# The filler matmuls between the stages of a block stack: left out of the norms

## The chip, the cores and the metric

One Trainium2 chip, of which the kernel uses one core. The metric is the device time of the whole program in microseconds. Before the change it is 2915.89 us, the median of three runs (2914.72 to 2917.57).

## The reference

512 tokens of width 1024 in float32 go through two layers of a first block and one layer of a second. Each layer is a feed-forward network, a token mix, and another feed-forward network, every one of them added to the running `x` after a norm:

```
h = modulate(rms_norm(x, g), shift, scale)
x = x + 0.5 * gate * (silu(h @ w_g) * (h @ w_u)) @ w_out        # feed-forward, inner width 2816
x = x + gate * token_mix(h)                                     # projections, spatial gating, sparse attention
```

with `rms_norm(x, g) = x * rsqrt(mean(x*x) + 1e-6) * g`. The second block has the same frame with a recurrent unit and two attentions in its mix, and no modulation. A final norm of the first block stands between the two. A norm needs all of `x`: no product of a stage can start before the norm ahead of it has given its first tile.

## The kernel before, in words

`x` lies transposed in SBUF, as 8 tiles of 128 features by 512 tokens. Every float32 product is done as three float32r matmuls (`pe_3`, lines 318 to 320): the high part of the weights times the high part of the data, high times low, low times high. Weights stream in as units, ScalarE makes their high part (line 290) and VectorE or GpSimd their low part (lines 283, 259). All engines run programs written out in order by hand and meet at counting semaphores; there is no scheduler.

The class `Norm` is one norm between two stages; this document calls the place of one a seam. Its order on TensorE is `pe_sum`, then `pe_spread`:

- The squares of `x` are made on ScalarE (line 389) and seven of eight tiles are added up on VectorE (line 398) while the stage before is still multiplying. `pe_sum` sums over the features with four one-column products of the accumulated tile (line 407) and, once the last tile of squares is there, four more (line 414). They are plain float32, and the trace shows each as two matmuls. Then `keep_warm` issues `warm[1]` matmuls of a constant 128x128 tile with 512 columns (line 313).
- VectorE and ScalarE turn the 512 sums into reciprocal roots (lines 424, 429, 436, and 569 to 576).
- `pe_spread` waits for them, spreads each over the 128 partitions with four products against the identity (line 442), and `keep_warm` issues `warm[2]` more.
- VectorE multiplies `x` by that (line 454), ScalarE makes the high part `hH` of each tile (line 487) and VectorE the low part `hL` (line 461, or 464 without a shift). TensorE starts the stage's products on tile 0 as soon as its `hL` is there, and takes one more tile at a time after that.

The products of `keep_warm` write PSUM bank 2, which nobody reads before the stage overwrites it; nothing waits for them.

The norms are numbered 0 to 9. Norm 0 (`warm=(26, 0, 16)`), the norm of the memory (6), the bridge between the blocks (7) and norm 8 (each `warm=(0, 0, 0)`) name their counts; at 7 and 8 products of a side stage stand where the filler would be. Norms 1, 2, 3, 4, 5 and 9 take the default `warm=(0, 4, 4)`. Their sums start at 397.2, 631.0, 998.9, 1366.9, 1601.3 and 2542.0 us of the profiled execution; they are called seams A to F here. A and D lead into the mix, C and the others into feed-forward networks (B, E, F in front of the second one of a layer, where VectorE also does the two halves of a low part, line 274, between its steps of the norm). `pe_woven`, the first group of products of the program, has its own filler matmuls (line 668).

Of the kernel before, what the change touches and what calls it, by code (L numbers as in the profile page):

```python
# [25 lines left out]
T = 512  # L26
# [332 lines left out]
class Norm:  # L359
# [4 lines left out]
    ADDS = 6  # L364
    SQUARES = KD + 1

    def __init__(self, n, q, a, y0=None, seam=None, tokens=T, src=None, warm=(0, 4, 4), warm_bank=2, banks=(6, 5, 7)):
        self.seam = seam
        self.warm, self.warm_bank, self.banks = warm, warm_bank, banks
        self.n, self.q, self.a, self.y0, self.tokens, self.src = n, q, a, y0, tokens, src or (lambda m, d: m.x[:, d])  # L370
# [2200 lines left out]
```

## Time and profile before

| | |
|---|---|
| median of 3 runs | 2915.89 us (2914.72 to 2917.57) |
| profiled execution, its own time | 2915.27 us |
| its span, first to last instruction | 2913.2 us |
| TensorE busy | 2875.0 us, 99% |
| VectorE, ScalarE, GpSimd busy | 53%, 29%, 8% |
| mean granted TensorE clock | 0.994 |

"PE" is TensorE, "PEld" its weight loads, "DVE" VectorE, "ACT" ScalarE. The granted clock is a share of 2.4 GHz: 1.00 is that, 0.50 is 1.2 GHz. The matmuls are pipelined, so a busy time holds the tail of each: what a matmul costs in a row of them is the distance from its start to the next one's start. In a row "[1.55 <-DVE m_hL L461]" says that the engine was idle for 1.55 us before it and what ended that.

### The profile page before, as it was taken

The numbers are of one execution on the slowest core, as the hardware profiler recorded it, in microseconds if no ns is written. First come the engines' busy times: TensorE is split into PE (matmuls) and PEld (weight loads), VectorE is DVE, ScalarE is ACT, GpSimd is POOL, SyncE is SP. The second block draws the span as 40 slices with busy tenths as digits, with TensorE's granted clock in tenths as the row PEclk, the third lists the DMA queues.
The fourth block names the chain that finished last, engine by engine and source line by source line (L and its number), as shares of the span: only waits on it lengthen the run. The fifth ranks groups of instructions, "written<-read, shape, count | busy, mean of one in ns | idle before, by whom it ended". The sixth has DMA issues, their size and how long they took to land.

```text
span 2913.2 us, 35989 instructions
## 1 busy us (share of the span) xinstructions
PE 2875.0 (99%) x13895; PEld 2372.3 (81%) x13895; DVE 1550.6 (53%) x2217; ACT 855.6 (29%) x998; POOL 237.4 (8%) x107
## 2 busy tenths in 40 slices
PE   8999999999999999999999999999999999999999
PEld 6888887878888888887887788888888878788887
DVE  7654658766533465365686662364423456643232
ACT  4222233442212322123334321243212344432121
POOL 0000005410000000000451000000000014100000
PEclk9999999999999999999999999999999999999999
DMA  6544522125523255353321462222322321123222
GB/s 264 197 159 157 196 98 94 51 88 181 194 72 112 78 186 202 113 183 120 112 69 59 162 220 95 104 105 80 117 82 89 115 89 44 62 99 128 72 96 77
DMA packets 63756, 351.23 MB, mean 121 GB/s; under 512 B 7842, under 2 KB 10274, under 8 KB 36260
## 3 DMA queue, kind: packets, MB, share of 16 engines
q1 hardware_dynamic: 62564, 347.90, 33.5%
q10 hardware_dynamic: 1088, 1.97, 0.4%
q8 instruction: 62, 1.02, 0.1%
q14 instruction: 42, 0.34, 0.0%
HBM read 345.78 MB, written 2.10 MB: 119 GB/s over the span
## 4 chain that ended last, share of the span: by engine, by line
PE 89%; DVE 6%; DVEq 2%; issue 1%; DMA 1%; ACT 1%; SPq 0%; ACTq 0%
PE bank L318 28%; PE bank L320 28%; PE bank L319 28%; DVE m_m L1522 2%; DVEq L1521 1%; PE bank L1128 1%; PE bank L326 1%; PE bank L1105 1%; PE bank L1114 0%; PE bank L442 0%; DVE m_masks L1532 0%; DVE m_masks L1530 0%; DVE m_masks L1524 0%; DVE m_masks L1537 0%; DVE m_mod_big L2105 0%
## 5 line engine op out<-in xcount | busy, mean ns | idle before, releaser
L318 PE MATMUL bank<-m_hH,m_wH 128*128 128x512 f32 x2464 | 967.0, 392 | 13.6 <-DVE m_hL L461 6.4
L320 PE MATMUL bank<-m_hH,m_wL 128*128 128x512 f32 x2464 | 960.5, 390 | 0.0
L319 PE MATMUL bank<-m_hL,m_wH 128*128 128x512 f32 x2464 | 960.2, 390 | 0.0
L283 DVE TENSOR_TENSOR m_wL<-m_wraw,m_wH 128x2048 fp32r<-128x2048 f32 (+3 forms) x185 | 459.9, 2486 | 583.6 <-ACT m_wH L290 583.0
L290 ACT ACTIVATE m_wH<-m_wraw 128x2048 fp32r<-128x2048 f32 (+3 forms) x236 | 459.7, 1948 | 897.4 <-PE bank L320 896.4
L318 PEld LDWEIGHTS bank<-m_hH,m_wH 128*128 128x128 f32 x2464 | 463.4, 188 | 114.5 <-issue 20.3
L320 PEld LDWEIGHTS bank<-m_hH,m_wL 128*128 128x128 f32 x2464 | 463.3, 188 | 97.3
L319 PEld LDWEIGHTS bank<-m_hL,m_wH 128*128 128x128 f32 x2464 | 463.7, 188 | 94.4 <-issue 0.2
L318 PE MATMUL bank<-m_guH,m_wH 128*128 128x512 f32 x1248 | 491.7, 394 | 3.6 <-DVE m_x L1197 2.8
L320 PE MATMUL bank<-m_guH,m_wL 128*128 128x512 f32 x1248 | 485.9, 389 | 0.0
L319 PE MATMUL bank<-m_guL,m_wH 128*128 128x512 f32 x1248 | 485.9, 389 | 0.0
L318 PEld LDWEIGHTS bank<-m_guH,m_wH 128*128 128x128 f32 x1248 | 234.1, 188 | 61.5 <-issue 9.8
L320 PEld LDWEIGHTS bank<-m_guH,m_wL 128*128 128x128 f32 x1248 | 234.2, 188 | 49.1
L319 PEld LDWEIGHTS bank<-m_guL,m_wH 128*128 128x128 f32 x1248 | 234.3, 188 | 46.6
L713 ACT ACTIVATE m_sg<-bank 128x512 f32<-128x512 f32 x132 | 78.7, 599 | 442.0 <-PE bank L320 441.7
L1047 DVE CUSTOM_DVE_ANT_0 m_mod_w<-m_mod_w,m_c 128x1024 f32<-128x1024 f32 x144 | 171.1, 1223 | 25.6 <-DMA m_mod_w<-in_ada_w 11.8
L759 DVE TENSOR_TENSOR m_gut<-m_sg,bank 128x512 f32<-128x512 f32 x132 | 90.8, 688 | 155.4 <-PE bank L320 151.8
L993 DVE SCALAR_TENSOR_TENSOR m_x<-bank,m_gate,m_x 128x512 f32<-128x512 f32 (+1 forms) x68 | 48.3, 717 | 184.4 <-PE bank L320 183.6
L259 POOL TENSOR_TENSOR m_wL<-m_wraw,m_wH 128x1024 fp32r<-128x1024 f32 (+1 forms) x30 | 85.7, 2858 | 234.6 <-ACT m_wH L290 234.6
L763 DVE TENSOR_TENSOR m_guL<-m_gut,m_guH 128x512 f32 (+1 forms) x132 | 91.4, 693 | 16.7 <-issue 0.8
L993 DVE SCALAR_TENSOR_TENSOR m_x<-bank,m_x 128x512 f32<-128x512 f32 (+1 forms) x42 | 27.8, 665 | 133.4 <-PE bank L320 133.1
L2222 POOL MEMSET m_other<- 128x1024 f32 x2 | 1.9, 955 | 1172.9 <-DVE m_wL L283 1172.9
(280 smaller groups left out, 2115.0 us busy)
## 6 DMA issues: line engine op xcount, KB each, us to landing
m_wraw<-in_ffn_in SPq DMA_DIRECT2D x132, 1024.0 KB, 4.8
m_mod_w<-in_ada_w SPq DMA_DIRECT2D x144, 512.0 KB, 4.5
m_wraw<-in_ffn_out_a SPq DMA_DIRECT2D x24, 1536.0 KB, 8.3
m_wraw<-in_ffn_out_b SPq DMA_DIRECT2D x24, 1280.0 KB, 6.1
m_wraw<-in_mix SPq DMA_DIRECT2D x30, 1024.0 KB, 4.8
m_wraw<-in_mix SPq DMA_DIRECT2D x26, 512.0 KB, 3.5
m_mod_big<-in_ada_w SPq DMA_DIRECT2D x16, 512.0 KB, 12.2
m_x<-in_x SPq DMA_DIRECT2D x2, 1024.0 KB, 6.3
```

Of the source, the lines that this page charges most:

```text
L259: nc.gpsimd.tensor_tensor(m.wL[:, j, 0:size], m.wraw[:, j, 0:size], f(m.wH[:, j, 0:size]), ALU.subtract)\
L283: nc.vector.tensor_tensor(m.wL[:, j, 0:size], m.wraw[:, j, 0:size], f(m.wH[:, j, 0:size]), ALU.subtract).then_inc(s.low, 1)
L290: nc.scalar.activation(m.wH[:, j, 0:size], m.wraw[:, j, 0:size], ACT.Copy).then_inc(s.high, 1)
L318: nc.tensor.matmul(out, a[0], b[0], start=first, stop=False)
L319: nc.tensor.matmul(out, a[0], b[1], start=False, stop=False)
L320: return nc.tensor.matmul(out, a[1], b[0], start=False, stop=last)
L713: nc.scalar.activation(m.sg[:, j], m.bank[j][:], ACT.Silu).then_inc(s.silu, 1)
L759: nc.vector.tensor_tensor(m.gut[:, j], m.sg[:, j], m.bank[2 + j][:], ALU.mult).then_inc(s.ufree, 1)
L763: nc.vector.tensor_tensor(m.guL[:, tile + j], m.gut[:, j], f(m.guH[:, tile + j]), ALU.subtract).then_inc(s.gu, 1)
L993: nc.vector.scalar_tensor_tensor(out=m.x[:, d, at], in0=m.bank[4 + d % 4][:, at], scalar=gate(d), in1=m.x[:, d, at], op0=ALU.mult, op1=ALU ...
L1047: return nc.vector.tensor_tensor_reduce(out=w, in0=w, in1=m.c[:], scale=1.0, scalar=0.0, op0=ALU.mult, op1=ALU.add, accum_out=m.red[:, k:k ...
L1522: nc.vector.max(m.m8[:], score[i])
```

## The change

The default of `warm` becomes `(0, 0, 0)`. At the six seams A to F no matmuls of `keep_warm` are issued any more, neither behind the sums nor behind the spreading. Nothing else changes: no wait, no buffer, no other count.

```diff
@@ -364,7 +364,7 @@ class Norm
-    def __init__(self, n, q, a, y0=None, seam=None, tokens=T, src=None, warm=(0, 4, 4), warm_bank=2, banks=(6, 5, 7)):
+    def __init__(self, n, q, a, y0=None, seam=None, tokens=T, src=None, warm=(0, 0, 0), warm_bank=2, banks=(6, 5, 7)):
```

## Rows read from the trace of the kernel before

**Rows 1.** The page: busy time, share and instructions; the chain that ended last.

```profile
PE 2875.0 (99%) x13895; PEld 2372.3 (81%) x13895; DVE 1550.6 (53%) x2217; ACT 855.6 (29%) x998; POOL 237.4 (8%) x107
PE 89%; DVE 6%; DVEq 2%; issue 1%; DMA 1%; ACT 1%; SPq 0%; ACTq 0%
```

**Rows 2.** Line 313 alone, first of six seams: start:end, length, PE, PEld busy (count).

```profile
397.22:404.33 7.11, 2.35 (x8) 1.36 (x8) 1.00 0.00 0
...
```

**Rows 3.** Timeline of TensorE at seam A: start, length, instructions, [idle before].

```profile
397.22 0.95 PE L407 MATMUL bank<-m_ones,m_acc 128*128 128x1 f32 x8
398.40 1.05 PE L414 MATMUL bank<-m_ones,m_sq 128*128 128x1 f32 x8 [0.24 <-ACT m_sq L389]
399.32 1.18 PE L313 MATMUL bank<-m_warm 128*128 128x512 f32 x4
400.69 1.16 PE L442 MATMUL bank<-m_cst,m_nr 128*128 128x128 f32 x8 [0.20 <-DVE m_nr L576]
401.61 1.17 PE L313 MATMUL bank<-m_warm 128*128 128x512 f32 x4
404.33 0.47 PE L318 MATMUL bank<-m_hH,m_wH 128*128 128x512 f32 x1 [1.55 <-DVE m_hL L461]
```

**Rows 4.** Timeline of VectorE at seam A.

```profile
400.48 0.17 DVE L576 SCALAR_TENSOR_TENSOR m_nr<-m_nv,m_nt 128x4 f32<-128x4 f32 x1
...
```

**Rows 5.** Seams A to F, first sum to first product: length, busy by engine, granted clock.

```profile
397.22:404.33 7.11, 5.12 (x34) 4.03 (x32) 4.18 (x12) 3.35 (x6) 0.00 (x0) 1.00 0.00 0
631.02:639.65 8.63, 6.47 (x33) 5.04 (x32) 6.61 (x15) 4.20 (x6) 0.00 (x0) 0.80 0.27 84
998.92:1006.94 8.02, 6.63 (x34) 5.32 (x32) 4.17 (x12) 4.20 (x6) 0.00 (x0) 0.79 0.36 131
1366.92:1374.54 7.62, 6.41 (x33) 4.91 (x32) 4.17 (x12) 3.34 (x6) 0.00 (x0) 0.78 0.00 1
1601.30:1609.05 7.75, 5.12 (x33) 4.02 (x32) 6.61 (x15) 4.19 (x6) 0.00 (x0) 1.00 0.18 48
2542.00:2550.18 8.18, 6.45 (x34) 5.22 (x32) 6.26 (x14) 4.13 (x6) 0.00 (x0) 0.79 0.25 88
```

**Rows 6.** The stretches at half clock, same columns (PE busy first).

```profile
15.79:22.61 6.82, 5.92 (x18) 5.05 (x19) 6.41 (x13) 2.27 (x5) 0.00 (x0) 0.50 1.03 420
29.44:36.26 6.82, 5.86 (x14) 4.63 (x15) 6.72 (x9) 1.11 (x2) 0.00 (x0) 0.50 1.03 406
633.60:637.01 3.41, 3.03 (x12) 2.23 (x11) 2.31 (x7) 2.00 (x2) 0.00 (x0) 0.50 0.00 0
1002.24:1005.65 3.41, 3.26 (x12) 2.87 (x12) 1.24 (x3) 1.52 (x2) 0.00 (x0) 0.50 0.36 145
1370.88:1374.29 3.41, 2.89 (x11) 1.98 (x9) 2.05 (x3) 1.38 (x2) 0.00 (x0) 0.50 0.01 2
2446.08:2449.49 3.41, 3.41 (x11) 2.61 (x10) 3.26 (x5) 0.28 (x1) 1.39 (x1) 0.50 0.00 0
2545.07:2548.48 3.41, 2.96 (x12) 2.60 (x12) 2.23 (x6) 1.62 (x1) 0.00 (x0) 0.50 0.15 26
```

**Rows 7.** Timeline of TensorE at seam C.

```profile
1002.39 2.08 PE L442 MATMUL bank<-m_cst,m_nr 128*128 128x128 f32 x8 [0.20 <-DVE m_nr L576]
1004.12 1.87 PE L313 MATMUL bank<-m_warm 128*128 128x512 f32 x4
1006.94 0.47 PE L318 MATMUL bank<-m_hH,m_wH 128*128 128x512 f32 x1 [0.95 <-DVE m_hL L461]
```

**Rows 8.** Timeline of TensorE inside the mix of the second block.

```profile
2445.00 0.66 PE L1646 MATMUL bank<-m_cst,m_other 128*128 128x128 f32 x4 [2.19 <-ACT m_other L1605]
...
2446.70 0.63 PE L319 MATMUL bank<-m_hL,m_wH 128*128 128x512 f32 x1
2447.13 0.63 PE L320 MATMUL bank<-m_hH,m_wL 128*128 128x512 f32 x1
```

**Rows 9.** TensorE's waits: who waited for whom, total us, times, longest.

```profile
PE bank L318 <- DVE m_hL L461: 6.4, 5, 1.5
```

## The prediction

> **What bounds the kernel now.** I read the page first: TensorE is busy 99% of the span, and 89% of the chain that ended last is its products [rows 1]. Whatever delays the first product of a stage, or makes products slower, therefore goes into the time nearly one to one; the rest of the chain is a search on VectorE that starts only when TensorE's first products after a norm are done. Then I took the seams. At seam A [rows 3] the stage's last product gives way to the sums at 397.22 and the next stage's first product starts at 404.33. The seam is a chain over three engines: sums until 399.45, VectorE's last reciprocal root from 400.48 to 400.65 [rows 4], spreading from 400.69, then a tile of `x` through VectorE, ScalarE and VectorE until its low part `hL` is there. The filler matmuls lie in the two holes of this chain. Third, the granted clock of the six seams [rows 5] and the stretches in which it was 0.50, 1.2 in place of 2.4 GHz [rows 6]: with the filler in place the clock already falls at B, C, D and F, and stays up at A and E.
>
> **What goes, and what it frees.** Eight matmuls a seam [rows 2] (the other five seams have eight each too), 48 in all. Counted by their work this would be up to 48 x 1.18 / 4 = 14 us [rows 3]. None of it is on the path. At A the first four end (399.32 + 1.18 = 400.50) 0.19 us before the spreading, which waits for VectorE; the second four end at 402.78, 1.55 us before the first product, which waits for `hL` [rows 3]. At C, where the second four run at half clock, they end at 1005.99 and the first product still waits 0.95 us for `hL` [rows 7]. They are issued behind the sums and the spreading, so they delay neither signal. The direct gain is 0; from the other side it can hardly be more than the 0.2 us of idle before the spreading, whose weight load may have been held up a little, 6 x 0.2 = 1.2 us at most. SP, GpSimd, every wait and every buffer are untouched.
>
> **What late products cost now.** The clock fell 2.58, 3.32, 3.96 and 3.07 us after the first sum of B, C, D and F (633.60 - 631.02 and so on, rows 5 and 6), mean 3.23. That is about when the spreading starts, and it pays: 2.08 us at C against 1.16 at A [rows 3, 7]. So the first product comes later: C 8.02 against A 7.11, B 8.63 against E 7.75 (both with VectorE's extra work), D 7.62 against A 7.11 [rows 5]. A fall costs 0.91, 0.88, 0.51. At all four the clock was back at full before the first product or within its time: the half stretches lasted 3.41 us, and TensorE worked 2.89 to 3.26 us of each, a good part of it filler (at C from 1004.12 on, rows 7).
>
> **What they cost afterwards.** Without the filler TensorE does only sums and spreading between 397.2 and 404.3: from 399.45 to 400.69 it is idle (1.24 us), and from 401.85 to 404.33 (2.48 us). An idle time of 2.19 us was enough for a fall within the mix (2445.00 in [rows 8], the stretch from 2446.08 in [rows 6]), and B, C, D and F fell even with the filler. I take it that the clock falls at all six.
>
> (a) Late spreading at A and E, which are spared now: 2 x 0.9 = 1.8 us. At B, C, D and F this is paid already.
>
> (b) Products at half clock. A product there costs 0.43 us from start to start (2446.70 to 2447.13, rows 8) and half of that at twice the clock (the page's 2875 us over 13,895 matmuls gives 0.21, rows 1), so half of the time spent so is lost. How long does it last? Where TensorE had paused for about one us in the half stretch, it lasted 6.82 us (5.92 and 5.86 busy, the two early rows of rows 6). In the seams afterwards TensorE will have the spreading, 2.05 us, then 2.75 us of idle, so less work than in any stretch of rows 6. Lower end: 3.41 us as now, the clock is back before the first product and (b) is 0. Next: 6.82 us, so until 3.23 + 6.82 = 10.05 us after the first sum; the first product is at 8.1 (mean of B, C, D, F), 1.95 us run at half clock, 0.97 us lost. Upper end: one 3.41 us more, since even in 6.82 us there are only 2.05 + 1.95 = 4.0 us of work, less than the 5.9 of the two early ones: until 13.5, 5.4 us at half clock, 2.7 lost. I take the middle of the last two, 1.85 us, because the pause lies differently to the stretch from seam to seam. Six seams: 11.1 us. No slack takes the loss: TensorE waited for a tile's `hL` five times at the five seams A to E, the first tile's each time (6.4 us in all), and never for a later one [rows 9]; at full clock it is the later of the two already, and at half clock the more so.
>
> Sum: 1.8 + 11.1 = 12.9 us on the profiled execution's own 2915.27 (span 2913.2 and 2.1 around it) = 2928.2; that execution lies 0.6 us under the median of the runs, so **2928.8 us**.
>
> The Trainium skill bears on this (TensorE: Matmul & The Clock Gate, "Why this matters for your kernels"): it advises against idle gaps above some 3 us between bursts of matmuls, and by that rule gaps of 1.2 and 2.5 us would be harmless. That speaks against my sum. The trace does not agree: the gap of 2.19 us was followed by a fall [rows 8]. What is worked out from rows for this case is the third rival below.
>
> **Rivals.** *One stretch only.* The clock falls everywhere but is back after 3.41 us: only (a), 2917.7. For it: every half stretch after the first 40 us was so long [rows 6]. Against it: TensorE worked 2.89 us or more in each, and here it would be the 2.05 us of spreading.
>
> *Always the long one.* 6 x 2.7 + 1.8 = 18.0, so 2933.9; for it that the two early long stretches had more work than these will have.
>
> *The gaps are harmless, the other side.* If falls hang on something else than on the filler's work (on long idle times, say, or a matter of chance), they come no more often than now: 2915.9; and if the plain gaps of a seam never drop the clock, the late starts of B, C, D and F vanish, 0.9 x 3 + 0.5 = 3.2 us, which gives 2912.7. It decides from the point where a seam keeps granted clock 1.00 with the two gaps of 1.2 and 2.5 us. For it: A kept it, with gaps of 0.20 and 1.55 us. Against it: C fell with gaps of 0.20 and 0.95 us [rows 3, 7].
>
> **Chances.** A measurement of this kernel tells 0.2% (5.8 us) from no change. Forecast, 2922 to 2932: 0.62. Always long, to 2936: 0.18. One stretch only, 2917.7, within 0.2%: 0.09. Harmless, 0.11, nearly all of it within 0.2% too, 0.02 faster by more. So slower 0.80, same 0.18, faster 0.02. The range is 2918 to 2935: the lower end is the first rival, the upper the second with a fall that comes a little earlier.
>
> **What the changed profile would show.** Line 313 with 63 matmuls for 111; rows of seam A with 0.50 in the clock and the spreading at 2.1 us; the gap before the first product some 2.5 us or more; then products 0.43 us apart for 2 to 5 us at each seam, and the mean granted clock at about 0.988 for 0.994 (six stretches of 7 to 10 us for four of 3.4). VectorE's first `hL` comes 0.9 us later at A and E and not at C. I am wrong if the half stretches still last 3.4 us, or if the clock stays at 1.00 at A and E; and wrong in another way if the time is there but lies outside the 15 us behind the seams.

## The result

The changed kernel takes 2926.96 us, the median of six runs (2925.55 to 2930.3), against 2916.56 us for the kernel before in six (2914.51 to 2917.57): 10.4 us more by the medians. The ratio on record, 1.0038 with a 95% interval of 1.0027 to 1.0050, is not the ratio of these two medians (that is 1.0036); here and below the interval belongs to the ratio. The forecast was 2928.8 us (+12.9) and slower. Run once more beside another kernel, it took 2926.21 us against 2917.24, ratio 1.0036, interval 1.0022 to 1.0049.

The profiled execution took 2926.91 us, its span is 2924.9 us, 11.7 us more than before, and the mean granted clock is 0.989 for 0.994. The head of the page and line 313 alone:

```profile
span 2924.9 us, 35893 instructions
PE 2869.3 (98%) x13847; PEld 2368.7 (81%) x13847; DVE 1550.3 (53%) x2217; ACT 855.1 (29%) x998; POOL 237.4 (8%) x107
L313 PE MATMUL bank<-m_warm x63: 387/393/792, 3.3 to 53.2; 128*128 128x512 f32 x63
```

TensorE does 48 matmuls less, all others do the same work, and the program is longer. Seam A in the timeline of TensorE, to be held against [rows 3]:

```profile
397.67 0.95 PE L407 MATMUL bank<-m_ones,m_acc 128*128 128x1 f32 x8
398.86 1.05 PE L414 MATMUL bank<-m_ones,m_sq 128*128 128x1 f32 x8 [0.24 <-ACT m_sq L389]
401.15 1.16 PE L442 MATMUL bank<-m_cst,m_nr 128*128 128x128 f32 x8 [1.24 <-DVE m_nr L576]
404.78 0.77 PE L318 MATMUL bank<-m_hH,m_wH 128*128 128x512 f32 x1 [2.47 <-DVE m_hL L461]
405.34 0.63 PE L319 MATMUL bank<-m_hL,m_wH 128*128 128x512 f32 x1
```

The spreading comes 3.48 us after the first sum and the first product 7.11, both as before; only the idle times have grown, from 0.20 to 1.24 and from 1.55 to 2.47 us (the tail of a filler matmul used to count as busy). What is new is the length of the first product, 0.77 us for 0.47: it runs at half clock. Below, a fall is a change of the granted clock from 1.00 to 0.50, and a half stretch is the time that it then stays at 0.50. The six seams from the first sum to the first product, as in [rows 5]:

```profile
397.67:404.77 7.10, 3.16 (x25) 2.82 (x24) 4.16 (x12) 3.34 (x6) 0.00 (x0) 0.87 0.00 0
633.79:642.07 8.28, 3.68 (x26) 3.24 (x24) 6.61 (x15) 4.19 (x6) 0.00 (x0) 0.78 0.23 70
1002.71:1010.01 7.30, 3.35 (x25) 2.91 (x24) 4.17 (x12) 4.20 (x6) 0.00 (x0) 0.80 0.43 144
1371.17:1378.29 7.12, 3.16 (x26) 2.82 (x24) 4.17 (x12) 3.34 (x6) 0.00 (x0) 0.82 0.00 1
1606.92:1615.49 8.57, 3.97 (x26) 3.54 (x24) 6.61 (x15) 4.19 (x6) 0.00 (x0) 0.75 0.25 84
2552.50:2560.26 7.76, 3.66 (x26) 3.22 (x24) 6.26 (x14) 4.13 (x6) 0.00 (x0) 0.77 0.23 72
```

Their half stretches, as in [rows 6]:

```profile
402.86:409.69 6.83, 4.91 (x12) 3.88 (x13) 6.70 (x11) 3.95 (x6) 0.00 (x0) 0.50 0.00 0
638.39:645.20 6.81, 4.34 (x15) 3.39 (x14) 6.04 (x10) 3.35 (x5) 0.00 (x0) 0.50 0.73 269
1007.03:1013.84 6.81, 4.33 (x12) 3.29 (x12) 6.14 (x10) 3.63 (x6) 0.00 (x0) 0.50 0.04 14
1375.67:1382.48 6.81, 4.34 (x12) 3.35 (x11) 6.50 (x10) 3.55 (x5) 0.00 (x0) 0.50 0.00 1
1611.18:1621.42 10.24, 7.77 (x22) 6.24 (x23) 9.17 (x14) 5.23 (x8) 0.00 (x0) 0.50 0.55 207
2556.68:2563.48 6.80, 4.39 (x14) 3.44 (x14) 6.05 (x10) 3.48 (x6) 0.00 (x0) 0.50 0.43 154
```

All six seams fall, and each stretch is 6.8 or 10.2 us long where it was 3.4; it reaches 3.1 to 5.9 us into the products. Their price can be read off directly. These rows run from the first product of a seam to the start of the 48th (the columns count line 318 alone, one in three of the 48), of the kernel before for seams A and E:

```profile
404.33:415.10 10.77, 6.30 (x16) 2.97 (x16) 1.00 0.01 2
1609.05:1619.83 10.78, 6.32 (x16) 2.97 (x16) 1.00 0.39 163
```

and of the changed kernel for all six:

```profile
404.77:417.86 13.09, 7.32 (x16) 3.55 (x16) 0.81 0.17 56
642.07:654.32 12.25, 7.07 (x16) 3.35 (x16) 0.87 0.34 130
1010.01:1022.56 12.55, 7.08 (x16) 3.50 (x16) 0.85 0.07 12
1378.29:1391.01 12.72, 7.20 (x16) 3.50 (x16) 0.84 0.14 44
1615.49:1629.05 13.56, 7.57 (x16) 3.64 (x16) 0.78 0.36 134
2560.26:2572.57 12.31, 7.10 (x16) 3.36 (x17) 0.87 0.15 52
```

Before, the six such stretches take 64.6 us together (10.73 to 10.78 each), afterwards 76.5: 11.9 us lost in products. The seams ahead of them take 47.3 us before [rows 5] and 46.1 now: 1.2 us won back. Together +10.7 of the span's +11.7 us. The rest lies elsewhere and partly cancels: ahead of seam A the program is 0.45 us longer, between the products of C and the sums of D 0.6 us shorter, and between the products of E and the sums of F 1.3 us longer. In that last part, inside the mix of the second block, which the change does not touch, a half stretch that was 3.41 us long before (from 2388.05 on) is 6.83 us long now (from 2396.24 on), and the one from 2446.08 on in [rows 6] is gone.

### The profile page after: what moved, and what is told of

The parts are those of the page before. It is cut to its first block, busy times and chain, and to the rows that moved or that the text cites. A ratio compares the mean times of both kernels' runs of the same rounds, so it can differ in the third digit from the quotient of the medians.

```text
span 2924.9 us, 35893 instructions
## 1 busy us (share of the span) xinstructions
PE 2869.3 (98%) x13847; PEld 2368.7 (81%) x13847; DVE 1550.3 (53%) x2217; ACT 855.1 (29%) x998; POOL 237.4 (8%) x107
## 4 chain that ended last, share of the span: by engine, by line
PE 89%; DVE 7%; DVEq 2%; issue 1%; ACT 1%; DMA 0%; SPq 0%; ACTq 0%
PE bank L318 29%; PE bank L319 28%; PE bank L320 28%; DVE m_m L1522 2%; DVEq L1521 1%; PE bank L1128 1%; PE bank L326 1%; PE bank L1105 1%; DVE m_mod_big L2105 1%; PE bank L1114 0%; DVE m_masks L1532 0%; DVE m_masks L1530 0%; DVE m_masks L1524 0%; PE bank L442 0%; DVE m_masks L1537 0%
```

## The experiments

Each is timed against the kernel before on the same chip; the second column of the table is the difference of the two medians in us, the third the ratio with its 95% interval, most of them some 2.6 us (0.09%) to either side. The last column comes from one profile each: the six seams and the 48 products behind each, together, less the same in the profile of the kernel before (47.3 + 64.6 = 111.9 us). It leaves out what changes elsewhere in the program.

| kernel | us | ratio | at the seams, us |
|---|---|---|---|
| changed kernel again | +9.0 | 1.0036 (1.0022 to 1.0049) | +11.5 |
| e1: filler behind the sums only | +7.4 | 1.0025 (1.0016 to 1.0035) | +10.7 |
| e2: filler behind the spreading only | +1.3 | 1.0005 (0.9996 to 1.0014) | +6.3 |
| e3: both holes filled, 5 and 10 | -0.4 | 0.9999 (0.9990 to 1.0008) | +0.4 |
| e4: eight thin filler matmuls | +10.0 | 1.0043 (1.0030 to 1.0057) | +12.3 |
| e5: left out at seam A alone | +0.5 | 0.9999 (0.9990 to 1.0008) | +1.9 |
| e6: 1 inside the sums, 5 and 6 | -4.3 | 0.9982 (0.9973 to 0.9991) | -3.2 |
| e7: 3 inside the sums, 5 and 6 | -3.7 | 0.9988 (0.9979 to 0.9997) | -2.2 |
| e8: 0 and 8 | +1.9 | 1.0010 (1.0001 to 1.0020) | +2.6 |
| e9: 1 inside the sums, 4 and 4 | -3.9 | 0.9988 (0.9979 to 0.9997) | -2.7 |

**Do the matmuls count, or their work?** (e4)

```diff
     for _ in range(n):
-        nc.tensor.matmul(m.bank[bank][:], m.warm[:], m.warm[:].unsqueeze(1).to_broadcast([P, TT, P]), start=True, stop=True)
+        if n == 4:
+            nc.tensor.matmul(m.bank[bank][:, 0:16], m.warm[:], m.warm[:, 0:16], start=True, stop=True)
+        else:
+            nc.tensor.matmul(m.bank[bank][:], m.warm[:], m.warm[:].unsqueeze(1).to_broadcast([P, TT, P]), start=True, stop=True)
```

> The eight filler matmuls of each of the six seams are issued, but with 16 columns in place of 512. Theory (their work counts, not that they are issued): as the changed kernel, +8 to +13 us, half stretches of 6.8 us or more at all six seams. Rival (any stream of instructions on TensorE's queue keeps it ready): as the kernel before, within 2 us.

+10.0 us: as if they were not there, though all 48 and their weight loads are issued. The rival that any stream on the queue will do has fallen. All six seams have half stretches of 6.83 or 10.24 us in its profile; those of A and B:

```profile
400.48:410.72 10.24, 8.42 (x26) 7.10 (x27) 8.01 (x12) 4.40 (x7) 0.00 (x0) 0.50 0.00 0
639.41:646.24 6.83, 5.01 (x17) 4.08 (x16) 6.49 (x11) 3.62 (x6) 0.00 (x0) 0.50 0.80 302
```

**Which of the two groups?** (e1, e2, e8; one number changes, as `warm=(0, 4, 0)`, `warm=(0, 0, 4)`, `warm=(0, 0, 8)`)

> Filler behind the sums only: warm=(0, 4, 0). Theory (the filler's work decides how soon the clock is back, and products at half clock are the price): TensorE has as little to do behind the spreading as in the changed kernel, so the half stretches stay at 6.8 us or more and the time stays near it, +7 to +11 us on the kernel before. Rival 1 (the filler behind the sums is what keeps the clock up, by preventing the fall): near the kernel before, 0 to +3 us. Rival 2 (each of the two groups gives its half): about +5.

> Filler behind the spreading only: warm=(0, 0, 4). Theory: the clock falls at most or all of the six seams, but the filler is there to bring it back before or soon after the first product: +2 to +5 us on the kernel before, part of the half stretches at 3.4 us. Rival 1 (the filler behind the sums matters): +7 to +11 as the changed kernel. Rival 2: about +5.

> No filler behind the sums, eight behind the spreading (3.4 us at half clock, against a hole of 2.75). Theory: falls at five or six seams as with four there, but the clock comes back sooner, the first product waits up to 0.7 us for the filler where it runs at half clock: +0 to +3 us on the kernel before, the half stretches of 10.2 us at A and F shorter. Rival (the stretches of 10.2 us come from the missing filler behind the sums): they stay, +1 to +3 us.

By the times the group behind the spreading is worth most of it: with it alone the time is within the uncertainty of the kernel before (+1.3 us, less than the 2 to 5 that I had expected, though the interval reaches to +4.1), without it 7 us over. The profiles show less at the seams: of the 10.7 us that the changed kernel loses there, the group behind the spreading alone saves 4.4 (e2, whose profiled execution is 1.3 us over its median), the group behind the sums alone nothing. That e1's profiled execution still takes 3.8 us less than the changed kernel's comes from elsewhere: between the products of E and the sums of F, where norms 7 and 8 have no filler in any version, it is 3.0 us shorter (920.41 against 923.45 us), without the half stretch from 2396.24 on. e2 is 1.7 us shorter there than the kernel before. So the time of a variant moves by up to 3 us for what happens outside the six seams.

My time for e1 held, but not the picture behind it. With filler behind the sums five of the seven half stretches at the seams (D has two) are 3.4 us long, and four of these five come only after the first product. Seam C of e1, TensorE's timeline:

```profile
1006.19 1.16 PE L442 MATMUL bank<-m_cst,m_nr 128*128 128x128 f32 x8 [0.20 <-DVE m_nr L576]
1009.82 0.47 PE L318 MATMUL bank<-m_hH,m_wH 128*128 128x512 f32 x1 [2.47 <-DVE m_hL L461]
...
1010.81 0.43 PE L319 MATMUL bank<-m_hL,m_wH 128*128 128x512 f32 x1
1011.03 0.63 PE L320 MATMUL bank<-m_hH,m_wL 128*128 128x512 f32 x1
```

The clock goes down at 1011.02, 1.2 us after the products have begun, and up again at 1014.43. TensorE is in full work all that time (3.41 of 3.41 us busy in the stretch); what came before the fall is the idle time of 2.47 us. In the kernel before, a fall hits the spreading and filler and costs 0.5 to 0.9 us; here the same 3.41 us hit nothing but products and cost 1.6. So a fall has two prices, and part of what filler buys is only that the stretch lies where it is cheap.

In e2 three of the six seams have short stretches or none (B and D, and C). Eight behind the spreading (e8) bring five stretches of 3.4 us and one of 6.8, none of 10.2, as the theory had it; but the filler then holds the first product up, as seam C shows:

```profile
1003.70 2.08 PE L442 MATMUL bank<-m_cst,m_nr 128*128 128x128 f32 x8 [1.24 <-DVE m_nr L576]
1005.43 3.76 PE L313 MATMUL bank<-m_warm 128*128 128x512 f32 x8
1008.99 0.58 PE L318 MATMUL bank<-m_hH,m_wH 128*128 128x512 f32 x1
```

The product waits for nothing but the filler (no idle time before it) and comes 8.77 us after the first sum, not 8.02. Over the six seams eight filler matmuls cost 3.0 us more up to the first product than e2's four (50.0 against 47.0 us) and save 6.8 us in the products (64.4 against 71.2). By the times, +1.9 and +1.3 us, e8 is no better than e2 all the same.

**Is more filler better than before?** (e3, `warm=(0, 5, 10)`)

> Both holes filled: warm=(0, 5, 10), 15 filler matmuls a seam for 8. Theory: with the holes filled the clock falls more seldom than at four of six seams and is back at once where it does, but ten filler matmuls at half clock last 4.3 us and would then keep the first product waiting for about 1 us: between -3 and +2 us on the kernel before. Rival (filler is never on the path, and more of it only helps): -3 us. Rival (falls do not depend on the filler's work): same falls as before and +4 us for the overlong filler.

The same time as before, and the same number of falls: B, C, E and F, with a granted clock of 0.79 or 0.80 each. Seams A to C (first sum to first product):

```profile
398.13:405.24 7.11, 6.70 (x40) 5.34 (x39) 4.17 (x12) 3.35 (x6) 0.00 (x0) 1.00 0.00 0
632.03:640.54 8.51, 8.12 (x40) 6.51 (x39) 6.61 (x15) 4.20 (x6) 0.00 (x0) 0.80 0.22 73
999.84:1008.06 8.22, 7.98 (x40) 6.79 (x39) 4.38 (x12) 4.20 (x6) 0.00 (x0) 0.79 0.34 128
```

The time is inside my range, but neither "more seldom" nor "it only helps" holds, and the first product of C comes 0.2 us later than before, not 1. At seam C TensorE is shown busy for 7.98 of 8.22 us, and the clock falls 3.16 us after the first sum all the same. What is left as little work there is the two groups of sums: sixteen matmuls of one column in some two us. That was the next theory. (A and D of the same profile have the same sums and did not fall, so it can be a condition of a fall, not the whole of it.)

**One matmul inside the sums** (e6; e7 has 3 for 1; e9 has 1 and leaves `warm=(0, 4, 4)`)

```diff
         if between:
             between()
+        elif self.warm[1]:
+            keep_warm(nc, m, self.warm_bank, 1)
         for tt in range(tiles):
...
-    def __init__(self, n, q, a, y0=None, seam=None, tokens=T, src=None, warm=(0, 4, 4), warm_bank=2, banks=(6, 5, 7)):
+    def __init__(self, n, q, a, y0=None, seam=None, tokens=T, src=None, warm=(0, 5, 6), warm_bank=2, banks=(6, 5, 7)):
```

> One filler matmul also between the two groups of sums, where TensorE is idle for 0.24 us, 5 behind the sums, 6 behind the spreading: 12 a seam. Theory (the two us of sums count as next to no work, and are why the clock falls even with both holes filled): fewer falls than four of six, -1 to -3 us on the kernel before. Rival (the falls come by themselves): four falls as before, 0 us.

> Three filler matmuls between the two groups of sums, 5 behind the sums, 6 behind the spreading. The second group of sums comes 0.4 us later at each seam, +2.4 us by itself. Theory: no or one fall, -3.2 us, so -1 us on the kernel before. Rival (the falls come by themselves): four falls, +2.4 us.

> The kernel before with one filler matmul more a seam, between the two groups of sums; 4 behind the sums and 4 behind the spreading as before. Theory (the gap in TensorE's work around the sums starts the fall, and one matmul inside it is enough): at most one fall in six seams, -3 to -4.5 us on the kernel before, level with twelve a seam (-4.3). Rival (it was the larger number behind the sums and the spreading together with it): two to four falls, -2 to 0 us.

e6 takes 2911.66 us against 2915.95, 4.3 us less: faster than both kernels, the best of this study, and more than the 1 to 3 us expected. Each of its eleven runs (2909.70 to 2913.12) is below each of the 33 of the kernel before beside it (2913.25 to 2921.15). In its profile no seam falls; the windows of A and C:

```profile
398.76:405.87 7.11, 6.03 (x37) 4.70 (x36) 4.17 (x12) 3.34 (x6) 0.00 (x0) 1.00 0.00 0
999.68:1006.79 7.11, 6.02 (x37) 4.69 (x36) 4.17 (x12) 4.20 (x6) 0.00 (x0) 1.00 0.44 147
```

and the timeline of TensorE at C:

```profile
999.68 0.95 PE L407 MATMUL bank<-m_ones,m_acc 128*128 128x1 f32 x8
1000.49 0.47 PE L313 MATMUL bank<-m_warm 128*128 128x512 f32 x1
1000.87 1.05 PE L416 MATMUL bank<-m_ones,m_sq 128*128 128x1 f32 x8
1001.78 1.41 PE L313 MATMUL bank<-m_warm 128*128 128x512 f32 x5
1003.16 1.16 PE L444 MATMUL bank<-m_cst,m_nr 128*128 128x128 f32 x8
1004.07 1.63 PE L313 MATMUL bank<-m_warm 128*128 128x512 f32 x6
1006.79 0.47 PE L318 MATMUL bank<-m_hH,m_wH 128*128 128x512 f32 x1 [1.09 <-DVE m_hL L463]
```

The added matmul fits where TensorE waited 0.24 us for the last squares: the second sums start 1.19 us after the first, against 1.18 before (398.40 - 397.22, [rows 3]). e9 shows that this one matmul does most of it: 3.9 us less and one fall in six, without e6's larger groups. That fall is at seam E:

```profile
1598.69:1606.88 8.19, 6.58 (x34) 4.95 (x33) 6.61 (x15) 4.19 (x6) 0.00 (x0) 0.79 0.21 65
```

Three inside the sums (e7) keep all six seams up too, but hold the second sums back to 1.59 us after the first; the first product comes 7.41 us after the first sum at A and C, 0.3 later, where 7.11 is possible. I had priced this at 2.4 us over the six seams; it is 1.0 (45.1 against e6's 44.1 us), since B and E, where VectorE has its extra work, lose nothing. So e7 is 3.7 us faster where I had said 1.

One rival is left untested. In e6, e7 and e9 the added matmul brings work into the sums and also closes the idle time of 0.24 us ahead of the second group. A matmul of 16 columns in the same place would tell the two apart; none was run.

**Do the seams add up?** (e5: `warm=(0, 0, 0)` at seam A alone)

> The filler is left out at seam A alone (norm 1 of the first layer), the other five keep it. Theory (each seam pays by itself, 10.4 us over six): +1.7 us on the kernel before; in the profile the first product of seam A comes at the same 7.1 us after the first sum or 0.9 later, and the 48 products behind it take 1.3 to 2.8 us longer than 10.8. Rival (the seams are coupled: one fall brings the next, or the loss is a fixed cost of the change somewhere else): 0, or 5 us and more.

By the time this is open: +0.5 us by the medians, and the interval reaches from -2.9 to +2.3 us. The profile has the local price, seam A to its first product and on to the 48th:

```profile
397.48:404.58 7.10, 3.15 (x26) 2.82 (x24) 4.17 (x12) 3.34 (x6) 0.00 (x0) 0.88 0.00 0
404.58:417.74 13.16, 13.16 (x48) 10.66 (x49) 9.67 (x14) 4.60 (x7) 1.84 (x2) 0.81 0.17 59
633.68:641.43 7.75, 5.11 (x34) 4.02 (x32) 6.61 (x15) 4.19 (x6) 0.00 (x0) 1.00 0.19 44
1368.03:1375.14 7.11, 5.12 (x33) 4.02 (x32) 4.17 (x12) 3.34 (x6) 0.00 (x0) 1.00 0.00 1
1601.88:1610.47 8.59, 6.49 (x33) 5.05 (x32) 6.61 (x15) 4.19 (x6) 0.00 (x0) 0.80 0.26 83
```

13.16 us for 10.77, so 2.4 us lost as in the full change. But in the same execution B and D, with the filler of the kernel before, did not fall, which gives back some 1.4 us, and E, which had kept its clock before, fell and takes 0.8 us more. Together the six seams cost 1.9 us. Whether the change at A had a part in the others' falls is not shown: the kernel before was profiled once, and its own falls may differ from run to run.

**The changed kernel again** (e10, the change as it is)

> The changed kernel once more, on the chip of the run beside it: +10 us on the kernel before (2926.96 against 2916.56), half stretches of 6.8 us or more at all six seams whatever the seam's phase. If the falls were a matter of chance, the profile would show some seam without one and a time away from this by several us.

The time is +9.0 us. Again six falls in six, four stretches of 6.83 and two of 10.24 us (B and C). Which seam gets the long one changes from run to run; that each has a fall did not, in twelve cases.

## Why the prediction was right

**The filler frees nothing.** Right: at seam A the spreading and the first product stand where they stood to 0.01 us with eight matmuls less, and e4, with all of them issued but thin, is as slow as the change.

**The clock falls at all six seams.** Right, in both profiles of the changed kernel.

**(a) Late spreading at A and E, +1.8 us.** Mis-sized, and of the other sign: -1.2 us over the six seams. I had taken the moment of the fall from the kernel before, 3.23 us after the first sum on average. Without the filler it came 4.2 to 5.2 us after it (402.86 - 397.67 = 5.19 at A, 4.6, 4.3, 4.5, 4.3, 4.2 at the others), when the spreading was partly or wholly done. Why it came later is open. Only E paid in full (8.57 us against 7.75); at A the first product was not late at all. In the repeat the falls came at 2.2 to 5.1 us and the seams took about as long as before (47.4 us), so (a) is around zero and varies.

**(b) Products at half clock, 11.1 us.** Measured 11.9 in this profile and 11.4 in the repeat. The two lengths named, 6.8 and 10.2 us, are the ones that occur, five to one (four to two in the repeat). The mean loss is that of the forecast by two errors that cancel: the short case occurs more often than I took it, but costs 1.5 to 2.3 us and not 0.97, since it starts later and so reaches further into the products. The price of a product was a little off too: at full clock one takes 0.23 us from start to start (10.77 / 47), not the 0.21 that the page's totals gave, so a product at half clock loses 0.20 of its 0.43 us, not half. That (b) came so near is in part luck.

**The rivals.** "One stretch only" fell: no seam came back after 3.4 us. "Always the long one" fell: one in six. "The gaps are harmless" fell with the clock at A and E. On this the Trainium skill's advice (TensorE: Matmul & The Clock Gate, "Why this matters for your kernels") to mind idle gaps above some 3 us does not agree with these traces: no gap in a seam of the changed kernel is longer than 2.48 us, and every seam fell; in e3 seam C fell with no idle time over 0.24 us shown. In these traces the length of the longest gap did not tell which seam would fall.

**The measure.** The sum gave 12.9 us, the medians 10.4, and this one profile 11.7. In the profile the two terms are -1.2 and +11.9, where the sum had +1.8 and +11.1. The kernel before varies by 3 us over its six runs beside the change and by 7.9 us over the 74 beside the experiments (2913.25 to 2921.15), and this goes with its mean granted clock: the 4 of these runs with 0.995 take 2913.7 us on average, the 42 with 0.994 2915.9, the 21 with 0.993 2917.8, the 7 with 0.992 2920.0. So it is time at half clock that comes and goes; at which places is not on record, since the kernel before was profiled once.

## What to carry to other kernels

Filler on an engine that waits anyway is free as long as it ends before what the engine waits for, and what it buys is the clock of the useful work behind it: before taking it out or putting it in, look at the granted clock from the last product of one stage to well behind the first products of the next, not at the wait itself. Put it where TensorE looks busy but streams next to nothing (a group of one-column sums), a matmul at a time in holes it fits in; the one such matmul a seam was worth more here (e9, -3.9 us) than seven more elsewhere (e3, -0.4). Size it for half clock: a group that just fits at full clock holds the next stage up when the clock has already fallen.

## What the runs showed of the hardware that was not expected

- A fall can come when TensorE has been in full work for 1.2 us again: in e1, at 1011.02, with products from 1009.82 on and 2.47 us of idle before them. Reading only what the engine does at the moment of the fall misleads.
- Sixteen one-column float32 matmuls, shown as about 2 us of busy TensorE, did not always hold the clock: seam C of e3 fell with 7.98 of 8.22 us busy, and one 512-column matmul set among them (e9) brought the falls in the profile from four seams to one. Whether by its work or by closing the idle time of 0.24 us is open.
- Eight matmuls of 16 columns in a seam are worth nothing to the clock (+10.0 us), though each is shown with a busy time of 0.26 us against 0.39 for one of 512 columns.
- What is still open is why six seams of one execution fare so differently with the same work: C and D fell and A and E did not in the profile of the kernel before, and with the same filler E fell and D did not in e5's. That it hangs on the moment at which a seam comes is a guess; no run here set that moment.
